# VectorE and ScalarE order at the norm boundaries of a two-layer trunk, and evictions of W_o moved ahead of weight splits

## The chip, the cores and the metric

One core of one Trainium2 chip. The metric is the device time of one execution in microseconds (us); a figure for a kernel is the median of several executions.

## The reference, cut to what matters

Two layers run over 272 tokens (16 learned ones and 256 given ones) with a model width of 1024, all in float32. Each layer has three sub-layers, each inside a pair of norms:

```
h = h + 0.5 * rmsnorm(swiglu(rmsnorm(h, g_pre), w1, w2), g_post)        # first half step
hn = rmsnorm(h, g_mix_pre)
u_pool, q, k, v, gate_pool, gate_attn = split(hn @ w_in)
merged = sigmoid(gate_pool) * y_pool + sigmoid(gate_attn) * y_attn
h = h + rmsnorm(merged @ w_o, g_mix_post)
h = h + 0.5 * rmsnorm(swiglu(rmsnorm(h, g_pre2), w3, w4), g_post2)      # second half step
```

The place where one sub-layer's result is normed and added to the trunk h, and the next sub-layer's operand is made from h, is called a boundary here.

## The kernel before, in words

The trunk `h` lies as 8 tiles (k = 0 to 7) of 128 features x 272 tokens. A float32 product is formed on TensorE from three products of rounded parts: each weight and each operand is split in a high part and a low part (`w_hi`, `w_lo`, `x_hi`, `x_lo`), and `products` (L437 to L439) issues high times high, high times low, and low times high. ScalarE makes the high parts (`split_hi` L833 for weights, `x_high` L857 for the operand), VectorE the low parts as source minus high part (`split_lo` L1076, `x_low` L1140).

Weights arrive in units of 1 MB or less, in a ring of four slots that SyncE fills. A slot's `raw` copy is free when VectorE has made its low part, its `w_hi` and `w_lo` when TensorE has used them. The order of the work on each engine is written out by hand, and semaphores tie the engines.

A boundary goes as follows. TensorE ends the last output tile; ScalarE squares it (`square`, L843); TensorE sums the squares over the features with one-column matmuls (`sum_part`, L513), with matmuls of no use around the waits (`keep_warm`, L523); ScalarE takes a root, VectorE refines it (`post_rms`, L1121 to L1129); TensorE spreads it over the partitions (`spread_rms`, L528). Then `boundary` runs on VectorE. For each tile it issues `normed` (L1149: `tmp` from `y` in SBUF and the spread root in PSUM), the update of `h` (L1158: `tmp` plus `h`, both in SBUF) and `x_low` (L1140: from `h` and `x_hi`, both in SBUF). ScalarE's `pre_norm` makes `x_hi` of each tile and the square of it, for the next norm. GpSimd adds up these squares (`add_squares`, L1536 for the first two, L1539 after that, SBUF to SBUF). `sq` has two buffers, and a square from the third on waits until an add has read its buffer. TensorE's `deep_pair` takes the 8 operand tiles in turn, twelve matmuls for each, and begins tile k when `x_lo` k is there; of tile 0 it takes the products with `x_hi` first (L457, L458).

In this program the boundary comes five times: after the first half step, after W_o and after the second half step of layer 0, and after the first half step and W_o of layer 1. What comes last is another path that the change does not touch. After a W_o boundary, and after the second half step, the next feed-forward stage begins: ScalarE loads an activation table, splits a unit of weights (`split_hi`), VectorE splits the first half of it and then computes the mean square (`split_lo_between` with `mean_square`, L1083, L1114), GpSimd takes the power -0.5 (`inverse_rms`, L1543), and TensorE spreads it (L528) between two output tiles. After the first half step, W_in follows, where VectorE computes the mean square before it splits weights.

W_o (units 62 to 65, output tiles 0 to 7) runs on TensorE as a `deep_pair` of units 62 and 63 and then units 64 and 65. VectorE evicts with `take_y` (L1444), two tiles of `y` each, and between them makes the low parts of units 66 to 68, the first weights of the next stage; ScalarE does their high parts and squares `y`. The last tile is squared straight from PSUM. The partial sum on TensorE ahead of the last three matmuls of tile 7 waits for GpSimd's fifth add, the one with the square of tile 5.

The core of `boundary` is:

```
for k in range(KD):
    dve.wait_ge(t_ready, ...)          # normed(k)
    h[:, k] = ...                      # L1158
    if k >= 2:
        x_low(at, columns, k - 1)
    if k + 1 < KD:
        normed(k + 1)
    if k == 0:
        x_low(at, columns, 0)
x_low(at, columns, KD - 1)
```

Of the kernel before, what the change touches and what calls it, by code (L numbers as in the profile page):

```python
# [48 lines left out]
KD = D // P  # L49
# [26 lines left out]
T_KV, T_Q, T_POOL, T_GATE, T_PP, T_AP, T_WO = 52, 56, 64, 68, 84, 92, 100  # L76
TILES = 160
# [6 lines left out]
TR0 = FFN_LAG - 4  # L84

NORMS = 6
# [7 lines left out]
def adds_to(n):  # L94

    return n // 2 * sum(ADDS) + n % 2 * ADDS[0]
# [38 lines left out]
def landed_at(u, layer, more=0):  # L135

    upto = sum(unit_dmas(v) for v in range(u % RING, u + 1, RING))
    return (layer * SLOT_DMAS[u % RING] + upto + more) * 16


def trunk(nc, x, meta_tokens, norm_g, ffn_w_in, ffn_w_out, w_in, pool_w_grp, pool_scale, w_pool_proj,
          sinks, w_attn_proj, w_o, geometry, out):
    with ExitStack() as ctx:
        def sb(name, shape, dt=F32):
            return ctx.enter_context(nc.sbuf_tensor(name, shape, dt))

        def sem(name):
            return ctx.enter_context(nc.semaphore(name))
# [8 lines left out]
        y = sb("y", [P, KD, T])  # L157
# [91 lines left out]
        tile_read = sem("tile_read")  # L249
# [575 lines left out]
        def _(act):  # L825
            act.sem_inc(silu_done, 2)

            def split_hi(u, l, more=0):
                act.wait_ge(raw_landed[u % RING], landed_at(u, l, more))

                act.wait_ge(unit_done, l * UNITS + u + 1 + (more * 4))
                for w, hi, _ in split_parts(u, l=l):
                    last = act.activation(hi, w, ACT.Copy)  # L833
                last.then_inc(hi_done, 1)

            def square(n, m, src, ready, at):

                act.wait_ge(ready, at)
                if m < 2:
                    act.wait_ge(ssq_done, n + 1)  # L840
                else:
                    act.wait_ge(acc_done, adds_to(n) + max(1, m - 2))
                act.activation(sq[:, m % 2, :], src, ACT.Square).then_inc(sq_done, 1)  # L843
# [11 lines left out]
            def x_high(columns, h_before, k):  # L855
                act.wait_ge(h_ready, h_before + k + 1)
                act.activation(x_hi[:, k, :], h[:, k, :], ACT.Copy, scale=columns[:, k:k + 1]).then_inc(xhi_ready, 1)  # L857

            def pre_norm(n, columns, h_before):

                for k in range(KD):
                    x_high(columns, h_before, k)
                    square(n, k, h[:, k, :], h_ready, h_before + k + 1)

            def silus(f, l, pair, more=0):
# [134 lines left out]
            for l in range(DEPTH):  # L1000
                ffn(0, l)
                act.wait_ge(layer_consts, l + 2)
                pre_norm(l * NORMS + 2, g_cur[:, 2 * KD:3 * KD], l * 3 * KD + KD)
                act.preload_act_table(ACT.Exp)
                for u in range(41, 46):
                    split_hi(u, l)
                act.wait_ge(v_turned, l + 1)
                act.activation(v_tok[:, :, :], pT_bank[:, :].rearrange("p (b c) -> p b c", b=2), ACT.Copy
                               ).then_inc(v_ready, 1)
                act.activation(v_pair[:, :, :], pTm_bank[0:4 * META, KV_DIM:2 * KV_DIM].rearrange("p (j c) -> p j c", j=2),  # L1010
                               ACT.Copy)
                act.activation(v_meta[:, :], pTm_bank[0:META, 0:KV_DIM], ACT.Copy).then_inc(v_ready, 1)
                for u in range(46, 49):
                    split_hi(u, l)
                if meta_queries(l):
                    act.wait_ge(s0_step, l * S0_STEPS + S0_SHIFTED)
                    act.activation(s0[0:META, :, 0:META], s0[0:META, :, 0:META], ACT.Exp)
                    act.activation(stats0[:, 2, :], stats0[:, 1, :], ACT.Exp).then_inc(s0_exp, 1)
                for c in range(KD):
                    split_hi(49 + c, l)  # L1020
                    if c >= 1:
                        tanh(2 * c - 2, l)
                        tanh(2 * c - 1, l)
                        take_pT(2 * c - 2, l)
                    exps(2 * c, l)
                    exps(2 * c + 1, l)
                    if c >= 1:
                        take_pT(2 * c - 1, l)
                split_hi(57, l)
                tanh(2 * KD - 2, l)  # L1030
                tanh(2 * KD - 1, l)
                take_pT(HEADS - 2, l)
                split_hi(58, l)
                take_pT(HEADS - 1, l)
                split_hi(59, l)
                split_hi(60, l)
                for n in range(4):
                    split_hi(61 + n, l)
                    if n >= 1:
                        merge_hi(2 * n - 2, l)  # L1040
                        merge_hi(2 * n - 1, l)
                merge_hi(6, l)
                merge_hi(7, l)
                act.preload_act_table(ACT.Sqrt)
                split_hi(65, l)
                split_hi(66, l)
                for m in range(4):
                    square(l * NORMS + 3, m, y[:, m, :], tile_read, l * TILES + T_WO + m + 1 + TR0)
                split_hi(67, l)
                for m in range(4, 6):  # L1050
                    square(l * NORMS + 3, m, y[:, m, :], tile_read, l * TILES + T_WO + m + 1 + TR0)
                split_hi(68, l)
                square(l * NORMS + 3, 6, y[:, 6, :], tile_read, l * TILES + T_WO + 6 + 1 + TR0)
                last_square(l * NORMS + 3, bank[3], l * UNITS + U_WO + 4 + RING)
                take_root(l * NORMS + 3)
                pre_norm(l * NORMS + 4, g_cur[:, 4 * KD:5 * KD], l * 3 * KD + 2 * KD)
                act.preload_act_table(ACT.Silu)
                ffn(1, l)
                if l < DEPTH - 1:

                    pre_norm(l * NORMS + NORMS, g_next, l * 3 * KD + 3 * KD)
                    act.preload_act_table(ACT.Silu)
# [6 lines left out]
        def _(dve):  # L1069
# [3 lines left out]
            def split_lo(u, l, more=0):  # L1073
                dve.wait_ge(hi_done, l * UNITS + u + 1 + more)
                for w, hi, lo in split_parts(u, l=l):
                    last = dve.tensor_tensor(lo, w, hi.bitcast(F32), ALU.subtract)  # L1076
                last.then_inc(lo_done, 1)
# [59 lines left out]
            def x_low(at, columns, k):  # L1137

                dve.wait_ge(xhi_ready, at + k + 1)
                dve.scalar_tensor_tensor(out=x_lo[:, k, :], in0=h[:, k, :], scalar=columns[:, k:k + 1],  # L1140
                                         in1=x_hi[:, k, :].bitcast(F32), op0=ALU.mult, op1=ALU.subtract
                                         ).then_inc(xlo_ready, 1)

            def boundary(n, l, at, columns):

                def normed(k):
                    dve.scalar_tensor_tensor(out=tmp[:, k % 2, 0:T], in0=y[:, k, :],  # L1149
                                             scalar=g_cur[:, (2 * n + 1) * KD + k:(2 * n + 1) * KD + k + 1],  # L1150
                                             in1=small[:, S_BC:S_BC + T], op0=ALU.mult, op1=ALU.mult
                                             ).then_inc(t_ready, 1)

                dve.wait_ge(bcast_done, l * NORMS + 2 * n + 2)
                normed(0)
                for k in range(KD):
                    dve.wait_ge(t_ready, l * 3 * KD + n * KD + k + 1)
                    dve.scalar_tensor_tensor(out=h[:, k, :], in0=tmp[:, k % 2, 0:T], scalar=1.0 if n == 1 else 0.5,  # L1158
                                             in1=h[:, k, :], op0=ALU.mult, op1=ALU.add).then_inc(h_ready, 1)
                    if k >= 2:  # L1160
                        x_low(at, columns, k - 1)
                    if k + 1 < KD:
                        normed(k + 1)
                    if k == 0:
                        x_low(at, columns, 0)
                x_low(at, columns, KD - 1)

            def take_gate(f, l, unit, mp=0):

# [213 lines left out]
            for l in range(DEPTH):  # L1383
# [55 lines left out]
                merge_lo(7, l)  # L1439
                split_lo(65, l)  # L1440

                def take_y(n):
                    b = 2 * (n % 2)
                    take(U_WO + n, F_WO + n, l, (b, b + 1), lambda j, ps: dve.tensor_copy(y[:, 2 * n + j, :], ps),  # L1444
                         (l * NORMS + 4) * KD if n == 3 else None, (lambda: split_lo(68, l)) if n == 3 else None)

                take_y(0)
                take_y(1)
                split_lo(66, l)
                split_lo(67, l)  # L1450
                take_y(2)
                take_y(3)
                post_rms(3, l)
# [210 lines left out]
```

## Time and profile before

| | us |
|---|---|
| median of 3 runs | 1229.23 |
| lowest and highest | 1226.35, 1229.56 |
| the profiled execution, its own time | 1229.71 |
| its span in the trace | 1227.6 |
| TensorE matmuls busy | 1200.9 (98%) |
| VectorE busy | 738.3 (60%) |
| ScalarE busy | 538.9 (44%) |
| GpSimd busy | 449.9 (37%) |

The time of the execution is the span and some 2 us around it. Busy times are sums over instructions, and TensorE's are modelled ends of pipelined matmuls. The boundaries' first `normed` starts at 224.74, 422.93, 630.78, 838.72 and 1028.57 us of the span.

### The profile page before, as it was taken

How to read it: one execution, taken by the hardware profiler on the slowest of the kernel's cores; microseconds unless marked ns; L12 is line 12 of the kernel's file. 1: busy time of each engine (PE TensorE's matmuls, PEld its weight loads, DVE VectorE, ACT ScalarE, POOL GpSimd, SP SyncE). 2: the span in 40 equal slices, each digit the busy share in tenths (PEclk: the TensorE clock that was granted, in tenths of full speed). 3: DMA queues.
4: the chain of work that ended last, by engine and by line, in shares of the span. 5: the costliest groups of instructions: out<-in, count | busy, mean ns of one | idle time of the engine just before them, and what ended most of it. 6: DMA issues, size and time to landing. Idle time of an engine off the chain costs nothing.

```text
span 1227.6 us, 23903 instructions
## 1 busy us (share of the span) xinstructions
PE 1200.9 (98%) x9364; PEld 1165.2 (95%) x9364; DVE 738.3 (60%) x1020; ACT 538.9 (44%) x747; POOL 449.9 (37%) x527
## 2 busy tenths in 40 slices
PE   6999999999999999999999999999999999999997
PEld 5999999999899999999999999999988998999986
DVE  4755444768866575553467554447678766755543
ACT  5433334535654453334344333345366645443441
POOL 2645411204512266452117454112054123755600
PEclk9999999999999899999999999999999999999999
DMA  9655356473256455534646553564733663664540
GB/s 286 207 171 162 119 171 205 116 231 104 70 138 206 137 165 179 171 120 152 206 139 207 171 162 117 171 205 117 232 104 83 167 198 104 212 199 155 169 173 35
DMA packets 197597, 197.58 MB, mean 161 GB/s; under 512 B 4120, under 2 KB 190720, under 8 KB 197520
## 3 DMA queue, kind: packets, MB, share of 16 engines
q1 hardware_dynamic: 197232, 196.22, 50.7%
q8 instruction: 56, 0.92, 0.3%
q10 hardware_dynamic: 288, 0.27, 0.1%
q14 instruction: 21, 0.17, 0.0%
HBM read 195.42 MB, written 1.05 MB: 160 GB/s over the span
## 4 chain that ended last, share of the span: by engine, by line
PE 86%; DVE 6%; ACT 4%; issue 2%; POOL 1%; DMA 0%; SPq 0%; DVEq 0%; ACTq 0%; POOLq 0%
PE bank L437 26%; PE bank L439 25%; PE bank L438 25%; ACT w_hi L833 2%; PE bank L619 2%; PE bank L620 2%; PE bank L618 2%; DVE w_lo L1076 2%; PE bank L513 1%; PE bank L523 1%; DVE s L1300 1%; DVE x_lo L1140 1%; DVE stats L1304 1%; DVE h L1158 1%; PE bank L707 1%
## 5 line engine op out<-in xcount | busy, mean ns | idle before, releaser
L1076 DVE TENSOR_TENSOR w_lo<-raw,w_hi 128x2048 fp32r<-128x2048 f32 (+3 forms) x208 | 439.0, 2116 | 285.3 <-ACT w_hi L833 285.3
L437 PE MATMUL bank<-x_hi,w_hi 128*128 128x272 f32 (+1 forms) x2028 | 589.2, 291 | 6.4 <-DVE w_lo L1076 4.4
L439 PE MATMUL bank<-x_hi,w_lo 128*128 128x272 f32 (+1 forms) x2028 | 582.6, 287 | 0.0
L438 PE MATMUL bank<-x_lo,w_hi 128*128 128x272 f32 (+1 forms) x2028 | 580.8, 286 | 0.0
L833 ACT ACTIVATE w_hi<-raw 128x2048 fp32r<-128x2048 f32 (+2 forms) x212 | 355.6, 1686 | 446.9 <-PE bank L439 435.1
L437 PEld LDWEIGHTS bank<-x_hi,w_hi 128*128 128x128 f32 x2028 | 383.2, 189 | 10.6 <-DVE w_lo L1076 4.8
L438 PEld LDWEIGHTS bank<-x_lo,w_hi 128*128 128x128 f32 x2028 | 383.2, 189 | 0.3
L439 PEld LDWEIGHTS bank<-x_hi,w_lo 128*128 128x128 f32 x2028 | 383.1, 189 | 0.0
L437 PE MATMUL bank<-hid_hi,w_hi 128*128 128x272 f32 x528 | 152.9, 290 | 0.0
L438 PE MATMUL bank<-hid_lo,w_hi 128*128 128x272 f32 x528 | 152.2, 288 | 0.0
L439 PE MATMUL bank<-hid_hi,w_lo 128*128 128x272 f32 x528 | 151.5, 287 | 0.0
L1554 POOL TENSOR_TENSOR hid_hi<-silu,up_r 128x272 f32 x88 | 76.3, 867 | 176.4 <-DVE up_r L1181 163.6
L1559 POOL TENSOR_TENSOR hid_lo<-hid_f,hid_hi 128x272 f32 x88 | 118.4, 1345 | 19.9 <-POOL hid_f L1556 19.9
L1556 POOL TENSOR_TENSOR hid_f<-silu,up_r 128x272 f32<-128x272 f32 x88 | 102.2, 1162 | 0.0
L438 PEld LDWEIGHTS bank<-hid_lo,w_hi 128*128 128x128 f32 x528 | 99.4, 188 | 0.0
L439 PEld LDWEIGHTS bank<-hid_hi,w_lo 128*128 128x128 f32 x528 | 99.3, 188 | 0.0
L437 PEld LDWEIGHTS bank<-hid_hi,w_hi 128*128 128x128 f32 x528 | 99.2, 188 | 0.0
L1539 POOL TENSOR_TENSOR acc<-acc,sq 128x272 f32<-128x272 f32 x56 | 44.3, 791 | 120.9 <-ACT sq L843 118.0
L1536 POOL TENSOR_TENSOR acc<-sq 128x272 f32<-128x272 f32 x11 | 14.6, 1328 | 169.6 <-ACT sq L843 169.6
L1181 DVE TENSOR_TENSOR up_r<-bank,r 128x272 f32<-128x272 f32 x88 | 37.7, 436 | 56.2 <-PE bank L439 56.2
L1174 DVE TENSOR_TENSOR gate_r<-bank,r 128x272 f32<-128x272 f32 x88 | 37.5, 434 | 38.3 <-PE bank L439 38.1
L1590 POOL TENSOR_TENSOR acc<-s,stats 128x16 f32<-128x16 f32 x64 | 18.9, 295 | 89.9 <-DVE stats L1317 89.9
(185 smaller groups left out, 1252.5 us busy)
## 6 DMA issues: line engine op xcount, KB each, us to landing
raw<-in_ffn_w_in SPq DMA_DIRECT2D x88, 1024.0 KB, 5.1
raw<-in_w_in SPq DMA_DIRECT2D x24, 1024.0 KB, 5.5
raw<-in_ffn_w_out SPq DMA_DIRECT2D x24, 768.0 KB, 4.4
raw<-in_ffn_w_out SPq DMA_DIRECT2D x24, 640.0 KB, 4.0
raw<-in_ffn_w_out SPq DMA_DIRECT2D x10, 1024.0 KB, 5.1
raw<-in_w_in SPq DMA_DIRECT2D x16, 512.0 KB, 4.8
raw<-in_w_attn_proj SPq DMA_DIRECT2D x32, 256.0 KB, 4.4
raw<-in_w_o SPq DMA_DIRECT2D x8, 1024.0 KB, 5.3
```

What stands on the lines that cost most here:

```text
L437: pe.matmul(ps[:, t0:T], w[0], a_hi[:, t0:T], start=start, stop=False)
L438: pe.matmul(ps[:, t0:T], w[0], a_lo[:, t0:T], start=False, stop=False)
L439: return pe.matmul(ps[:, t0:T], w[1], a_hi[:, t0:T], start=False, stop=stop)
L618: pe.matmul(ps[:, :], hid_hi[:, k, cols], w[0], start=k == 0, stop=False)
L833: last = act.activation(hi, w, ACT.Copy)
L1076: last = dve.tensor_tensor(lo, w, hi.bitcast(F32), ALU.subtract)
L1174: dve.tensor_tensor(gate_r[:, j, :], bank[4 * (unit // 2 % 2) + j][:, 0:T], r[:, :], ALU.mult).then_inc(tile_read, 1)
L1181: dve.tensor_tensor(up_r[:, j, :], bank[2 + j][:, 0:T], r[:, :], ALU.mult).then_inc(tile_read, 1)
L1539: pool.tensor_tensor(acc[:, :], acc[:, :], sq[:, m % 2, :], ALU.add).then_inc(acc_done, 1)
L1554: pool.tensor_tensor(hid_hi[:, ds(i * 2 + j, 1), :].rearrange("p o t -> p (o t)"), silu[:, j, :], up_r[:, j, :], ALU.mult).then_inc(hid_hi ...
L1556: pool.tensor_tensor(hid_f[:, j, :], silu[:, j, :], up_r[:, j, :], ALU.mult).then_inc(hf_ready, 1)
L1559: pool.tensor_tensor(hid_lo[:, ds(i * 2 + j, 1), :].rearrange("p o t -> p (o t)"), hid_f[:, j, :], hid_hi[:, ds(i * 2 + j, 1), :].rearrang ...
```

## The change: what it does, and the diff

Three things move; no instruction is added or taken away. In `pre_norm` ScalarE makes `x_hi` of tile k+1 before it squares tile k. In `boundary` VectorE updates `h` of tiles 0 and 1 before it makes `x_lo` 0, and from then on makes `x_lo` k in the same round as the update of `h` k, behind `normed` k+1. In W_o the low part of unit 67 goes from ahead of tile 4 to behind tile 6, and ScalarE's high part of unit 67 from ahead of the square of tile 4 to behind that of tile 5, and the square of tile 6 ahead of the high part of unit 68.

```diff
 def pre_norm(n, columns, h_before):
+    x_high(columns, h_before, 0)
     for k in range(KD):
-        x_high(columns, h_before, k)
+        if k + 1 < KD:
+            x_high(columns, h_before, k + 1)
         square(n, k, h[:, k, :], h_ready, h_before + k + 1)
...
 # ScalarE, W_o
-split_hi(67, l)
 for m in range(4, 6):
     square(l * NORMS + 3, m, ...)
+split_hi(67, l)
+square(l * NORMS + 3, 6, ...)
 split_hi(68, l)
-square(l * NORMS + 3, 6, ...)
...
 # VectorE, boundary
-    if k >= 2:
-        x_low(at, columns, k - 1)
+    if k == 1:
+        x_low(at, columns, 0)
     if k + 1 < KD:
         normed(k + 1)
-    if k == 0:
-        x_low(at, columns, 0)
-x_low(at, columns, KD - 1)
+    if k >= 1:
+        x_low(at, columns, k)
...
 # VectorE, W_o
+def split_two():
+    split_lo(67, l)
+    split_lo(68, l)
 def take_y(n):
-    take(..., (lambda: split_lo(68, l)) if n == 3 else None)
+    take(..., split_two if n == 3 else None)
 take_y(0)
 take_y(1)
 split_lo(66, l)
-split_lo(67, l)
 take_y(2)
 take_y(3)
```

On VectorE, the boundary before (`tmp` is `normed`, `h` the update, `x_lo` the low part):

```order
L1149 SCALAR_TENSOR_TENSOR tmp<-y,g_cur,bank 128x272
L1158 SCALAR_TENSOR_TENSOR h<-tmp,h 128x272
L1149 SCALAR_TENSOR_TENSOR tmp<-y,g_cur,bank 128x272
L1140 SCALAR_TENSOR_TENSOR x_lo<-h,g_cur,x_hi 128x272
L1158 SCALAR_TENSOR_TENSOR h<-tmp,h 128x272
L1149 SCALAR_TENSOR_TENSOR tmp<-y,g_cur,bank 128x272
L1158 SCALAR_TENSOR_TENSOR h<-tmp,h 128x272
L1140 SCALAR_TENSOR_TENSOR x_lo<-h,g_cur,x_hi 128x272
L1149 SCALAR_TENSOR_TENSOR tmp<-y,g_cur,bank 128x272
L1158 SCALAR_TENSOR_TENSOR h<-tmp,h 128x272
```

and the same place now (lines have moved by two):

```order
L1151 SCALAR_TENSOR_TENSOR tmp<-y,g_cur,bank 128x272
L1160 SCALAR_TENSOR_TENSOR h<-tmp,h 128x272
L1151 SCALAR_TENSOR_TENSOR tmp<-y,g_cur,bank 128x272
L1160 SCALAR_TENSOR_TENSOR h<-tmp,h 128x272
L1142 SCALAR_TENSOR_TENSOR x_lo<-h,g_cur,x_hi 128x272
L1151 SCALAR_TENSOR_TENSOR tmp<-y,g_cur,bank 128x272
L1142 SCALAR_TENSOR_TENSOR x_lo<-h,g_cur,x_hi 128x272
L1160 SCALAR_TENSOR_TENSOR h<-tmp,h 128x272
L1151 SCALAR_TENSOR_TENSOR tmp<-y,g_cur,bank 128x272
L1142 SCALAR_TENSOR_TENSOR x_lo<-h,g_cur,x_hi 128x272
```

Before, a round from tile 2 on is `h` k, `x_lo` k-1, `normed` k+1; now it is `h` k, `normed` k+1, `x_lo` k, so that `h` k+1 comes directly behind `x_lo` k.

On VectorE in W_o before (the first row is the low part of unit 65):

```order
L1076 TENSOR_TENSOR w_lo<-raw,w_hi 128x2048
L1444 COPY y<-bank 128x272 x4
L1076 TENSOR_TENSOR w_lo<-raw,w_hi 128x2048 x2
L1444 COPY y<-bank 128x272 x3
L1076 TENSOR_TENSOR w_lo<-raw,w_hi 128x2048
L1444 COPY y<-bank 128x272
```

and now:

```order
L1078 TENSOR_TENSOR w_lo<-raw,w_hi 128x2048
L1449 COPY y<-bank 128x272 x4
L1078 TENSOR_TENSOR w_lo<-raw,w_hi 128x2048
L1449 COPY y<-bank 128x272 x3
L1078 TENSOR_TENSOR w_lo<-raw,w_hi 128x2048 x2
L1449 COPY y<-bank 128x272
```

One weight split of 128x2048 has gone from ahead of the three evictions of tiles 4, 5 and 6 to behind them.

## Rows read from the trace of the kernel before

**Rows 1.** The page, part 4: share of the span by engine in the chain.
```profile
PE 86%; DVE 6%; ACT 4%; issue 2%; POOL 1%; DMA 0%; SPq 0%; DVEq 0%; ACTq 0%; POOLq 0%
```

**Rows 2.** Waits of PE: us in total, times, longest us.
```profile
PE bank L437 <- DVE x_lo L1140: 1.5, 4, 0.4
...
PE bank L513 <- POOL acc L1539: 1.1, 2, 0.9
```

**Rows 3.** Timeline, VectorE, first boundary: start, duration (us), instruction, idle before.
```profile
224.74 0.50 DVE L1149 SCALAR_TENSOR_TENSOR tmp<-y,g_cur,bank 128x272 f32<-128x272 f32 x1 [0.64 <-PE bank L528]
...
226.36 0.50 DVE L1140 SCALAR_TENSOR_TENSOR x_lo<-h,g_cur,x_hi 128x272 fp32r<-128x272 f32 x1 [0.24 <-ACT x_hi L857]
226.78 0.43 DVE L1158 SCALAR_TENSOR_TENSOR h<-tmp,h 128x272 f32<-128x272 f32 x1
...
228.02 0.49 DVE L1140 SCALAR_TENSOR_TENSOR x_lo<-h,g_cur,x_hi 128x272 fp32r<-128x272 f32 x1
...
230.29 0.52 DVE L1158 SCALAR_TENSOR_TENSOR h<-tmp,h 128x272 f32<-128x272 f32 x1
230.74 1.00 DVE L1140 SCALAR_TENSOR_TENSOR x_lo<-h,g_cur,x_hi 128x272 fp32r<-128x272 f32 x1
...
232.18 0.66 DVE L1158 SCALAR_TENSOR_TENSOR h<-tmp,h 128x272 f32<-128x272 f32 x1
...
236.75 0.50 DVE L1140 SCALAR_TENSOR_TENSOR x_lo<-h,g_cur,x_hi 128x272 fp32r<-128x272 f32 x1 [0.18 <-ACT x_hi L857]
```

**Rows 4.** Timeline, ScalarE, the same boundary.
```profile
225.81 0.52 ACT L857 ACTIVATE x_hi<-h,g_cur 128x272 fp32r<-128x272 f32 x1 [2.57 <-DVE h L1158]
...
227.25 0.52 ACT L857 ACTIVATE x_hi<-h,g_cur 128x272 fp32r<-128x272 f32 x1 [0.60 <-DVE h L1158]
```

**Rows 5.** Timeline, GpSimd, the same boundary.
```profile
228.17 0.97 POOL L1536 TENSOR_TENSOR acc<-sq 128x272 f32<-128x272 f32 x1 [22.22 <-ACT sq L843]
229.74 1.70 POOL L1539 TENSOR_TENSOR acc<-acc,sq 128x272 f32<-128x272 f32 x2 [0.60 <-ACT sq L843]
231.77 0.77 POOL L1539 TENSOR_TENSOR acc<-acc,sq 128x272 f32<-128x272 f32 x1 [0.33 <-ACT sq L843]
```

**Rows 6.** Timeline, TensorE, the same boundary: tile 5 begins; the sum behind tile 7.
```profile
235.11 0.39 PE L437 MATMUL bank<-x_hi,w_hi 128*128 128x272 f32 x1
...
239.73 0.72 PE L513 MATMUL bank<-ones,acc 128*128 128x1 f32 x6
```

**Rows 7.** Timeline, GpSimd and VectorE, a feed-forward stage of layer 0.
```profile
39.67 0.78 POOL L1559 TENSOR_TENSOR hid_lo<-hid_f,hid_hi 128x272 f32 x1 [0.23 <-POOL hid_f L1556]
...
39.72 2.87 DVE L1076 TENSOR_TENSOR w_lo<-raw,w_hi 128x2048 fp32r<-128x2048 f32 x1 [1.61 <-ACT w_hi L833]
```

**Rows 8.** Timeline, behind the W_o boundary of layer 0: ScalarE, GpSimd, TensorE.
```profile
435.17 1.28 ACT L1057 ACT_TABLE_LOAD   x1
...
439.79 1.77 POOL L1543 TENSOR_TENSOR rt<-var,half 128x3 f32<-128x3 f32 x1 [3.79 <-DVE var L1114]
...
441.62 0.54 PE L528 MATMUL bank<-ident,rt 128*128 128x128 f32 x3
```

**Rows 9.** Timeline, VectorE, W_o of layer 0: unit 67, ahead of tile 4.
```profile
411.14 2.29 DVE L1076 TENSOR_TENSOR w_lo<-raw,w_hi 128x2048 fp32r<-128x2048 f32 x1 [3.31 <-ACT w_hi L833]
```

**Rows 10.** Last sum and first `normed` of three boundaries; one stretch (third last column: PEclk).
```profile
222.11 0.83 PE L513 MATMUL bank<-ones,sq 128*128 128x1 f32 x6 [0.49 <-ACT sq L843]
...
418.59 1.31 PE L513 MATMUL bank<-ones,sq 128*128 128x1 f32 x6 [0.49 <-ACT sq L843]
...
422.93 0.50 DVE L1149 SCALAR_TENSOR_TENSOR tmp<-y,g_cur,bank 128x272 f32<-128x272 f32 x1 [1.85 <-PE bank L528]
...
1025.15 0.83 PE L513 MATMUL bank<-ones,sq 128*128 128x1 f32 x6 [0.49 <-ACT sq L843]
...
1028.57 0.50 DVE L1149 SCALAR_TENSOR_TENSOR tmp<-y,g_cur,bank 128x272 f32<-128x272 f32 x1 [1.42 <-PE bank L528]
...
420.00:422.00 2.00, 2.00 (x10) 2.00 (x11) 0.73 (x5) 0.20 (x1) 0.00 (x0) 0.50 0.88 293
```

More of the change, by code:

```diff
@@ L1048, in _ @@
                     square(l * NORMS + 3, m, y[:, m, :], tile_read, l * TILES + T_WO + m + 1 + TR0)
-                split_hi(67, l)
                 for m in range(4, 6):
                     square(l * NORMS + 3, m, y[:, m, :], tile_read, l * TILES + T_WO + m + 1 + TR0)
+                split_hi(67, l)
+                square(l * NORMS + 3, 6, y[:, 6, :], tile_read, l * TILES + T_WO + 6 + 1 + TR0)
                 split_hi(68, l)
-                square(l * NORMS + 3, 6, y[:, 6, :], tile_read, l * TILES + T_WO + 6 + 1 + TR0)
                 last_square(l * NORMS + 3, bank[3], l * UNITS + U_WO + 4 + RING)
@@ L1444, in take_y @@
                     take(U_WO + n, F_WO + n, l, (b, b + 1), lambda j, ps: dve.tensor_copy(y[:, 2 * n + j, :], ps),
-                         (l * NORMS + 4) * KD if n == 3 else None, (lambda: split_lo(68, l)) if n == 3 else None)
+                         (l * NORMS + 4) * KD if n == 3 else None, split_two if n == 3 else None)
                 take_y(0)
```

## The prediction

> **What bounds the kernel now.** I read the page first, then TensorE's waits, then the five boundaries on the timeline of each engine, and last W_o and the granted clock around it. In the chain that ended last TensorE has 86%, and VectorE and ScalarE together 10% [rows 1]: a change on those two is worth only what TensorE stops or starts to wait for. The list of waits shows how little that is. The waits for `x_lo` come to 1.5 us, and the waits of W_o's partial sum for GpSimd's adds to 1.1 us [rows 2]. So the gain is small whatever happens, and the question is what the new order does to engines that had a margin.
>
> At a boundary I take the first `normed` as time 0 (224.74 at the first [rows 3]). TensorE then needs an `x_lo` for each 12 matmuls, and three tiles and the slow first matmul take 239.73 - 235.11 = 4.62, or 1.54 a tile [rows 6]. Before, `x_lo` 1 ends at 3.77 and `x_lo` 7 at 12.51 [rows 3], TensorE's sum behind tile 7 comes at 14.99 [rows 6].
>
> **A lock between VectorE and GpSimd.** Three durations in the boundary are not those of their kind. An `x_lo` takes 0.49 and once 1.00, an update of `h` 0.43 and once 0.66 [rows 3]. GpSimd's add takes 0.77 and once 0.97 [rows 5]. The ends explain them. The add of 231.77 ends at 232.54 and the update of 232.18 at 232.84, 0.30 later. The pair of adds ends at 231.44 and the long `x_lo` at 231.74, again 0.30 later. The add of 0.97 ends at 229.14, which is 0.77 behind 228.37, and the `x_lo` beside it ends at 228.51, 0.14 later. So an update or an `x_lo` (two operands in SBUF) and an add run one after the other: VectorE lets go 0.14 before its recorded end, and an instruction of VectorE that had to wait ends 0.30 behind the add. `normed`, with one operand in PSUM, I take as free.
>
> **The new order, stepped through.** I count from the end of an update of `h` k. `x_hi` k starts 0.04 later (227.21 to 227.25 [rows 3, 4]), and `x_lo` k 0.55 behind that start (225.81 to 226.36), so at 0.59. The next update now stands directly behind `x_lo` and is issued 0.42 after it (226.36 to 226.78), at 1.01. On ScalarE the square of tile k-1 now follows `x_hi` k, and GpSimd's add for it starts 0.92 behind the start of `x_hi` (227.25 to 228.17 [rows 4, 5]), at 0.96. `x_lo` lets go at 0.59 + 0.49 - 0.14 = 0.94. So the add arrives when the lock is free, 0.05 ahead of the update, and holds it: the add ends at 1.73 and the update at 2.03. The next round repeats this. **A round takes 2.03 us, and TensorE needs one each 1.54 us.** Before, `x_lo` k-1 and `normed` stood between two updates, and the adds fell beside `normed` in most rounds.
>
> Does 0.05 decide? In the feed-forward stages GpSimd starts 0.02 to 0.05 ahead of a weight split 26 times. The first is the row of 39.67: the split, issued at 39.72, takes 2.87 [rows 7] where one alone takes 2.29 [rows 9], and the multiply keeps its 0.78. All 26, the last at 1059.18, go this way. And the second add of the pair began 0.77 before 231.44, at 230.67, 0.14 before the end of the update at 230.81 and ahead of the `x_lo` of 230.74 [rows 3, 5]: GpSimd does get in between two instructions of VectorE that follow each other.
>
> The opening of the new boundary is better than before: updates 0 and 1 end at 0.96 and 1.84, `x_lo` 1, behind `x_lo` 0 and `normed` 2, at 3.07 (0.70 sooner), `x_lo` 2 at 4.51. The first add, at 4.39, then meets update 3, due at 4.43: the add ends at 5.16, the update at 5.46, `x_lo` 3 at 5.46 + 0.59 + 0.49 = 6.54. From there `x_lo` 4 to 7 end 2.03 apart, at 8.57, 10.60, 12.63 and 14.66. TensorE ends one tile behind the last: 14.66 + 0.06 + 1.6 = 16.3, or **1.4 us later** than 14.99.
>
> **What follows a boundary.** Update 7 ends at 13.58, `x_hi` 7 starts at 13.62, and two squares follow it, 0.4 each: ScalarE is done at about 14.80, where before the table load began at 435.17 - 422.93 = 12.24 [rows 8, 10]. Behind it hang the table load, the high part, half a low part, the mean square and GpSimd's power, which ended at 441.56, and TensorE spread it at 441.62 [rows 8]. This path had no margin, and now it is 14.8 - 12.2 = 2.6 later. So at the three boundaries into a feed-forward stage (two W_o, one second half step) TensorE is **2.5 us** later and not 1.4. At the two into W_in the mean square waits for TensorE's sum alone, and 1.4 stands. Sum: 2 x 1.4 + 3 x 2.5 = **+10.3 us**.
>
> **W_o.** Unit 67's low part (2.29 [rows 9]) leaves the place ahead of tile 4. Tiles 4 and 5 are evicted when TensorE has them, their squares and adds come some 3 us sooner, and the partial sum waits for no add: **-1.1 us** [rows 2]. The square of tile 6 comes some 2 us sooner too. The moved splits end near 418.4 in layer 0, and the eviction of tile 7 follows the last square as before. Units 67 and 68 are first used after the boundary. SyncE loads the unit that follows 67 some 2.6 us later, into a slot that is not used for over 20 us. I cost these at nothing, with that time as cover.
>
> **The clock.** From 420.00 to 422.00 the granted clock is 0.50, so 1.2 GHz in place of 2.4 [rows 10], after TensorE had only one-column matmuls and short waits for most of 416 to 419. From the last sum to the first `normed` the first boundary takes 224.74 - 222.11 = 2.63, the W_o boundaries 4.34 and 3.42 [rows 10]. The surplus of 1.7 and 0.8 is the clock's. The change shortens the sparse stretch by 0.2 and 0.9 and shifts it in time. Between 0 and -2.5 I take half, **-1.2 us**. The Trainium skill ("TensorE: Matmul & The Clock Gate", What's actually happening) has the clock fall back only after an idle window; by that no wait here, of 0.9 at most [rows 2], would lower it, nothing could be won, and the sum would be 1238.9. The trace disagrees with it, since the clock did fall.
>
> **Sum.** The profiled execution took 1229.7, half a microsecond above the median of 1229.23. 1229.7 + 10.3 - 1.1 - 1.2 = 1237.7; against the median I say **1237.5 us**. A measurement of this kernel can tell about 0.3%, or 3.7 us, from no change.
>
> **The rivals.** *VectorE first.* If the update wins against the add, a round takes 0.59 + 0.42 + 0.44 = 1.45, less than TensorE's 1.54, and the add has room beside `normed`. `x_lo` 7 would end at 11.7 in place of 12.5, for some -0.8 at each boundary into W_in, and ScalarE's last square at 11.85 in place of 12.24, for -0.4 at the three others. With W_o and the clock: 1229.7 - 1.6 - 1.2 - 1.1 - 1.2 = 1224.6, faster. It decides once the add arrives over 0.05 later against the update than the rows say. For it speaks how narrow that is; against it the 26 cases. The Trainium skill's page "SBUF — State Buffer", Who interferes with whom, has the first to issue hold the pair of ports for the whole instruction. By that `x_lo` would hold it until 1.08, the update be in the queue by then, and 1224.6 could result. The trace disagrees as to the last 0.14 of an instruction (the add at 230.67). *Mixed.* The race goes either way from tile to tile. Each lost one costs 0.6, five are run at each boundary, and at half of them lost the time is near 1231. *W_o gives nothing.* Were the sum's wait replaced by one for the square of tile 6, +1.1 and 1238.8; it lies inside the forecast.
>
> **Chances.** GpSimd first everywhere 0.72 (of which 0.25 for a clock that gives nothing, at 1238.9); VectorE first 0.18; mixed 0.10. The forecast's own range is 1234 to 1241: the clock's ends give +1.2 and -1.3; a boundary whose clock falls because TensorE now idles there would add 0.8 each, so some +2 more at the top; less delay behind the boundary than 2.5 takes 2 off. The range of 8 in 10 goes on down over the mixed case to 1225. Faster by over 0.3%: 0.19. Within: 0.06. Slower: 0.75.
>
> **What would show it.** In the new trace updates of `h` 3 to 7 last about 1.03 us in place of 0.44, `x_lo` ends come 2.03 apart, adds keep 0.77, TensorE waits for `x_lo` some 25 times (9 us or so in all), and for GpSimd's power by about 1 us three times; the wait for an add in W_o is gone. Updates of 0.44, 1.45 us apart, with adds stretched to about 1.0, would show the first rival. A forecast of slower is wrong if the last `x_lo` ends before 12.5 us after the first `normed`.

## The result, and the profile after

The changed kernel takes 1238.12 us (median of 4 runs, 1237.48 to 1238.68), where the kernel before took 1228.47 (median of 4, 1226.35 to 1229.56) beside it. The ratio is 1.0078, with a 95% interval from 1.0062 to 1.0094: slower by 0.8%. The profiled execution took 1237.94, with a span of 1235.8. The forecast was 1237.5.

TensorE's waits in the changed kernel (line, what it waited for: us in total, times, longest us):

```profile
PE bank L437 <- DVE x_lo L1142: 6.0, 23, 0.4
...
PE bank L528 <- POOL rt L1547: 3.2, 3, 1.2
PE bank L513 <- ACT sq L843: 2.4, 5, 0.5
...
PE bank L457 <- ACT x_hi L857: 1.5, 3, 0.6
PE bank L437 <- DVE kT L1391: 0.5, 1, 0.5
```

The waits for `x_lo` were 1.5 us and the waits for the adds in W_o 1.1 [rows 2]. The first are now 6.0 and the second are gone. Two others cost time now: the waits for GpSimd's power (`rt`), 3.2 us at three places where there were 0.3 at one, and one for the eviction of K (`kT`).

The timeline of VectorE at the first boundary (start, duration in us, instruction, idle before), where the first `normed` starts at 224.67:

```profile
227.68 0.43 DVE L1160 SCALAR_TENSOR_TENSOR h<-tmp,h 128x272 f32<-128x272 f32 x1
228.03 0.49 DVE L1151 SCALAR_TENSOR_TENSOR tmp<-y,g_cur,bank 128x272 f32<-128x272 f32 x1
228.70 0.50 DVE L1142 SCALAR_TENSOR_TENSOR x_lo<-h,g_cur,x_hi 128x272 fp32r<-128x272 f32 x1 [0.18 <-ACT x_hi L857]
229.12 1.02 DVE L1160 SCALAR_TENSOR_TENSOR h<-tmp,h 128x272 f32<-128x272 f32 x1
230.06 0.48 DVE L1151 SCALAR_TENSOR_TENSOR tmp<-y,g_cur,bank 128x272 f32<-128x272 f32 x1
230.73 0.50 DVE L1142 SCALAR_TENSOR_TENSOR x_lo<-h,g_cur,x_hi 128x272 fp32r<-128x272 f32 x1 [0.18 <-ACT x_hi L857]
231.15 1.01 DVE L1160 SCALAR_TENSOR_TENSOR h<-tmp,h 128x272 f32<-128x272 f32 x1
...
238.80 0.50 DVE L1142 SCALAR_TENSOR_TENSOR x_lo<-h,g_cur,x_hi 128x272 fp32r<-128x272 f32 x1 [0.59 <-ACT x_hi L857]
```

GpSimd beside it:

```profile
229.07 0.77 POOL L1540 TENSOR_TENSOR acc<-sq 128x272 f32<-128x272 f32 x1 [24.30 <-ACT sq L843]
231.09 0.76 POOL L1543 TENSOR_TENSOR acc<-acc,sq 128x272 f32<-128x272 f32 x1 [1.25 <-ACT sq L843]
```

Updates are counted from 0 by their tile, so the row of 227.68 is update 2. It takes 0.43. Update 3 is issued at 229.12, and the first add has started at 229.07, 0.05 earlier. The add takes its usual 0.77 and ends at 229.84. The update ends at 230.14, 0.30 later, so that it takes 1.02. From then on each update from tile 3 to tile 7 has its add about 0.05 ahead of it: the updates start 2.01 to 2.03 us apart and take 1.0. It is so at all five boundaries, for 25 of the 40 updates, and in none of these rounds do the two engines fall out of step. The median duration of all 40 updates is 1.00, where before it was 0.46.

TensorE at the end of that boundary, and the path of the power behind the W_o boundary of layer 0 (TensorE, ScalarE, GpSimd):

```profile
240.95 0.77 PE L513 MATMUL bank<-ones,acc 128*128 128x1 f32 x6
...
437.17 1.28 ACT L1059 ACT_TABLE_LOAD   x1
...
441.79 1.77 POOL L1547 TENSOR_TENSOR rt<-var,half 128x3 f32<-128x3 f32 x1 [3.21 <-DVE var L1116]
...
443.61 0.54 PE L528 MATMUL bank<-ident,rt 128*128 128x128 f32 x3 [1.02 <-POOL rt L1547]
```

The sum comes 240.95 - 224.67 = 16.28 us behind the first `normed`, not 14.99 [rows 3, 6]. At the second boundary the first `normed` is at 422.41, so the table load starts at 14.76, where it was 12.24 [rows 8, 10], and TensorE waits 1.02 for the power, where it did not wait at 441.62 [rows 8].

All five boundaries, measured in us from start to start on the timelines: A from TensorE's last sum to the first `normed` (2.63 where the clock holds), B from there to the sum behind tile 7, C from that sum to the spread of the next norm.

```
            boundary 1          2                   3                   4                   5
            A     B     C       A     B     C       A     B     C       A     B     C       A     B     C
before      2.63 14.99  3.69    4.34 14.93  3.76    2.63 14.94  3.83    2.63 15.01  3.50    3.42 14.79  3.92
changed     3.74 16.28  3.74    2.63 16.29  4.91    3.39 16.29  4.98    3.00 16.28  3.56    2.63 16.22  4.98
```

The difference of the spans, 8.2 us, comes apart so: B gives +6.7 and C +3.5, together **+10.2**. A, the clock's share, gives -0.3. From the spread of the next norm behind boundaries 1 and 4, with which C ends, to the first partial sum of W_o it is 0.0 and -0.35, and within W_o's sums -0.15. The first stage, ahead of everything that was changed, was 1.2 shorter in this execution.

### The profile page after: what moved, and what is told of

The parts are those of the page before. It is cut to its first block, busy times and chain, and to the rows that moved or that the text cites. A ratio compares the mean times of both kernels' runs of the same rounds, so it can differ in the third digit from the quotient of the medians.

```text
span 1235.8 us, 23903 instructions
## 1 busy us (share of the span) xinstructions
PE 1203.0 (97%) x9364; PEld 1164.8 (94%) x9364; DVE 744.6 (60%) x1020; ACT 539.2 (44%) x747; POOL 445.1 (36%) x527
## 4 chain that ended last, share of the span: by engine, by line
PE 82%; DVE 9%; ACT 5%; issue 3%; POOL 1%; DMA 0%; SPq 0%; DVEq 0%; ACTq 0%; POOLq 0%
PE bank L437 24%; PE bank L439 24%; PE bank L438 24%; DVE h L1160 2%; ACT w_hi L833 2%; DVE w_lo L1078 2%; PE bank L620 2%; PE bank L619 2%; PE bank L618 2%; DVE x_lo L1142 1%; ACT x_hi L857 1%; PE bank L513 1%; DVE s L1301 1%; PE bank L523 1%; DVE stats L1305 1%
```

## The experiments

Medians in us, each beside runs of the kernel before on the same chip. The changed kernel was not run again beside them, so a difference from its 1238.12 is one between sessions; the medians of the kernel before were 1228.47 beside the changed kernel, and 1229.35 to 1229.67 in the others. The diffs are cut short. "Stepped" in the expectations means the same walk through the order, with the same lock, as in the prediction.

**The boundary part alone.** W_o's evictions, splits and squares as before.

```diff
 # VectorE and ScalarE, W_o: the changed kernel's edit undone
-square 4, 5; split_hi(67); square 6; split_hi(68)
+split_hi(67); square 4, 5; split_hi(68); square 6
-take_y(0); take_y(1); split_lo(66); take_y(2); y 6; split_lo(67); split_lo(68); y 7
+take_y(0); take_y(1); split_lo(66); split_lo(67); take_y(2); y 6; split_lo(68); y 7
```

> The boundary part of the change alone (both engines' new order), W_o as before. Theory (GpSimd's add gets the lock 0.05 us ahead of the update of h): updates 3 to 7 of each boundary take 1.00 us, the sum behind tile 7 comes 16.3 us after the first normed instead of 14.9, TensorE waits about 1.2 us for GpSimd's power three times, and the time is 10 us above before, about 1238.5 us, since the W_o part gave back at most 1. Rival (most of the loss comes from W_o or from a clock that falls elsewhere): within 4 us of before.

Measured: 1241.23 against 1229.35, ratio 1.0097 (1.0078 to 1.0117). B is 16.2 to 16.3 at all five boundaries, and the waits for the power come to 3.2. The loss lies in the boundary. It is more than forecast, 11.9 and not 10. W_o, which is as before here, has no part in that. The traces show two things that I had not counted: between boundaries 1 and 4 and W_o 0.4 and 0.8 are lost, and the parts A are 3.0 longer in all than before. This kernel is 3.1 above the changed one; in the traces 1.7 of the difference is W_o's and 3.2 the parts A's, in an execution of 1243.15, 1.9 above its median.

**The W_o part alone.** The boundaries as before.

> The W_o part alone. Theory: the waits of the partial sum for the adds (0.20 and 0.94 us) go, -1.1 us, and the clock changes where it falls, -2 to +1: 1226.5 to 1229.5 us. Rival (the evictions moved ahead cost the next stage, so that the part loses): over 1230 us, with a new wait of TensorE for w_lo of unit 67 or 68.

Measured: 1226.83 against 1229.35, ratio 0.998 (0.9969 to 0.999), so some 2.5 us faster: within the range, and no wait for `w_lo` of a later unit appears. From the spread behind boundary 1 to the first partial sum of W_o it takes 172.34 in place of 172.74, and in layer 1 164.41 in place of 165.51: -1.5, with another -0.15 within the sums. The other 0.9 of the 2.5 lies in no path that I read; the interval reaches from -3.8 to -1.2.

**ScalarE as before, VectorE new.**

```diff
-x_high(columns, h_before, 0)
 for k in range(KD):
-    if k + 1 < KD:
-        x_high(columns, h_before, k + 1)
+    x_high(columns, h_before, k)
     square(n, k, ...)
```

> The change with ScalarE's order of before (x_hi k, then the square of k), VectorE's order new. Stepped through with the same lock rule: the add of tile k then arrives with x_lo k or just ahead of the next update, the rounds of 2.03 us begin one tile earlier (update 2 already takes about 1.0), the sum comes 16.9 us after the first normed, and the last square ends at 15.0: about 2 x 0.6 + 3 x 0.2 = 1.8 us above the changed kernel, near 1240 us. Rival (the new order of ScalarE, which puts the squares late, is what brings the add against the update): with the old order the updates take 0.44, and the time is near or below before.

Measured: 1238.97 against 1229.35, ratio 1.008 (1.006 to 1.01). B is 16.87, 16.85, 16.84, 16.85 and, at the last boundary, 15.66; the stepped figure was 16.9. The time is near that of the changed kernel (1238.12 in another session) and 1 below the expected one. The timelines of VectorE and GpSimd at the first boundary:

```profile
227.72 1.01 DVE L1158 SCALAR_TENSOR_TENSOR h<-tmp,h 128x272 f32<-128x272 f32 x1
...
229.74 1.01 DVE L1158 SCALAR_TENSOR_TENSOR h<-tmp,h 128x272 f32<-128x272 f32 x1
```

```profile
227.52 0.91 POOL L1538 TENSOR_TENSOR acc<-sq 128x272 f32<-128x272 f32 x1 [22.01 <-ACT sq L843]
229.69 0.77 POOL L1541 TENSOR_TENSOR acc<-acc,sq 128x272 f32<-128x272 f32 x1 [1.26 <-ACT sq L843]
```

Here update 2 already waits, and from update 3 on the add is again 0.05 ahead. The place of the squares is thus not what brings the adds against the updates. It is VectorE's order, in which an update follows `x_lo` directly.

The last boundary shows how narrow it is. The first add, GpSimd's first row above, starts beside an `x_lo`, 2.81 behind the first `normed`, at all five boundaries. At four of them it takes 0.91 and update 2 waits. At the last one update 2 gets in first:

```profile
1039.18 0.44 DVE L1158 SCALAR_TENSOR_TENSOR h<-tmp,h 128x272 f32<-128x272 f32 x1
1038.99 1.26 POOL L1538 TENSOR_TENSOR acc<-sq 128x272 f32<-128x272 f32 x1 [10.27 <-ACT sq L843]
```

The rounds of 2 us begin only at update 4 there. So in one kernel the same tie went both ways.

**The adds a little later.** Two memsets of 48 columns on GpSimd, of no use, ahead of each add of a pre-norm (not of the post-norm sums); all else as in the changed kernel.

```diff
+def linger(q):
+    if q % 2 == 0:
+        pool.memset(spare[:, 0:48], 0.0)
+        pool.memset(spare[:, 48:96], 0.0)
 ...
+linger(q)
 pool.tensor_tensor(acc[:, :], ..., ALU.add)
```

> The changed kernel with two small memsets on GpSimd ahead of each add of a boundary's pre-norm squares, so that the add comes 0.1 us or more later against the update of h. If the race for the lock is what costs the time, VectorE now comes first: updates take 0.44 and follow each other by 1.45 us, adds stretch to about 1.0 us, the sum comes about 13.9 us after the first normed, the last square ends at 11.85, and the time falls by some 13 us below the changed kernel, to 1224.5 (1222.5 to 1226.5), below before too. Rival (the loss comes from the waits of x_lo for x_hi in the new order, not from the lock): the memsets change nothing or cost 1 to 3 us more, 1238 to 1241 us.

Measured: 1223.68 (1223.23 to 1225.92) against 1229.35, ratio 0.9958 (0.9943 to 0.9972). **Work added to GpSimd takes 14.4 us off the changed kernel (15.3 if each is taken against the kernel before beside it), and the result is 5.7 below the kernel before.** Its timeline, VectorE and then GpSimd:

```profile
230.44 0.44 DVE L1161 SCALAR_TENSOR_TENSOR h<-tmp,h 128x272 f32<-128x272 f32 x1
230.79 0.49 DVE L1152 SCALAR_TENSOR_TENSOR tmp<-y,g_cur,bank 128x272 f32<-128x272 f32 x1
231.47 0.50 DVE L1143 SCALAR_TENSOR_TENSOR x_lo<-h,g_cur,x_hi 128x272 fp32r<-128x272 f32 x1 [0.18 <-ACT x_hi L858]
231.89 0.43 DVE L1161 SCALAR_TENSOR_TENSOR h<-tmp,h 128x272 f32<-128x272 f32 x1
```

```profile
231.81 0.14 POOL L1538 MEMSET spare<- 128x48 f32 x1 [0.22 <-ACT sq L844]
231.88 0.14 POOL L1539 MEMSET spare<- 128x48 f32 x1
231.98 0.98 POOL L1551 TENSOR_TENSOR acc<-acc,sq 128x272 f32<-128x272 f32 x1
```

The round is 231.89 - 230.44 = 1.45, the update takes 0.43, and now the add waits: it ends at 232.96, which is 0.77 behind 232.19, and the update ends at 232.32, 0.13 later. B is 13.7 to 13.9. The rival, by which the waits of `x_lo` for `x_hi` (0.18 a round, still there) cost the time, has fallen.

**How little later.** One memset of one column.

```diff
-        pool.memset(spare[:, 0:48], 0.0)
-        pool.memset(spare[:, 48:96], 0.0)
+        pool.memset(spare[:, 0:1], 0.0)
```

> The changed kernel with one memset of a single column ahead of each add, to see how narrow the race is. The add came 0.05 us ahead of the update. If the memset shifts it by more than that (a guess: 0.07), VectorE comes first in every round and the time is that of the longer delay, near 1224 us. If by less, nothing changes: 1238 us. A race that goes either way from round to round would give a time between, near 1231 us, with updates of both lengths.

Measured: 1223.67 (1223.3 to 1223.99) against 1229.58, ratio 0.9951 (0.9937 to 0.9966): level with the two longer memsets, and with them the fastest of the study. VectorE and GpSimd:

```profile
228.69 0.44 DVE L1161 SCALAR_TENSOR_TENSOR h<-tmp,h 128x272 f32<-128x272 f32 x1
```

```profile
228.61 0.10 POOL L1538 MEMSET spare<- 128x1 f32 x1 [23.14 <-ACT sq L844]
228.67 1.09 POOL L1546 TENSOR_TENSOR acc<-sq 128x272 f32<-128x272 f32 x1
```

The first `normed` is at 224.23 here, so the add starts 4.44 behind it, where it was 4.40 (229.07 - 224.67) in the changed kernel: a shift of 0.04 us in the record is enough, and at all five boundaries. The add's record even begins 0.02 ahead of the update's, and the update wins. In the same trace a multiply of GpSimd that starts at 143.01, 0.02 ahead of a weight split of 128x1280, is not held up (0.78), and the split takes 2.11 where the one of 549.48 in the kernel before takes 1.49. A start in the record tells who comes first only to some hundredths of a microsecond.

**The boundary part with the adds later.** W_o as before, one memset of one column.

> The boundary part alone, with the single-column memset ahead of each add, so that VectorE wins the race; W_o as before. It parts the gain of the new boundary from that of W_o. Theory: W_o is worth 2.5 us (the W_o part alone: 1226.8 against 1229.4), so about 1226.2 us, between 1225 and 1227.5, still some 3 us below before. Rival (the gain of the late adds depends on W_o's order too): outside that.

Measured: 1226.78 against 1229.67, ratio 0.9976 (0.9967 to 0.9986). The new boundary, with the race won by VectorE, gives 2.9 us of its own. With W_o's 2.5 that is 5.4, near the 5.9 of the kernel above. The memset ahead of the adds with the boundary's old order was not run, so how much of the 2.9 is the new order's is open: before, too, some instructions waited (`x_lo` of 1.00, updates of 0.66 [rows 3]).

**The mean square first.** The changed kernel, with the path behind the boundary shortened.

```diff
-split_lo_between(u0 + 3, l, lambda: mean_square(4 * f, l))
+mean_square(4 * f, l)
+split_lo(u0 + 3, l)
```

> The changed kernel, but at a feed-forward stage VectorE computes the mean square ahead of the first weight split and not between its halves. Theory (three boundaries lose 1.1 us each beyond the rounds, because the path over ScalarE's table load and weight split to GpSimd's power ends 2.6 us later): with the mean square off that path TensorE waits no more for the power, the 3.2 us of those waits go, and the time is near 1235 us. Rival (that time is lost anyway, since the weight splits are late too and TensorE then waits for w_lo or a bank): 1237 us or more, with new waits in place of the old.

Measured: 1238.55 against 1229.58, ratio 1.0069 (1.0054 to 1.0085): no gain. TensorE's waits:

```profile
PE bank L437 <- DVE x_lo L1142: 6.0, 23, 0.3
...
PE bank L437 <- DVE up_r L1182: 2.2, 3, 1.0
```

The waits for the power are gone, C is 3.6 to 3.8, and a wait for the eviction of the second unit (`up_r`) has come in their place: it stands behind two weight splits, which come from ScalarE as late as before. So my expectation failed and its rival held. The lateness of ScalarE's splits reaches TensorE by two paths, and to remove one uncovers the other. On the timelines the three boundaries with what follows them are 1.0 shorter in all; the median does not show it.

**Both.** The adds late (two memsets) and the mean square first.

> The adds late and the mean square first. If both effects are what they seem, they add: 1223.7 less the 2.3 us that TensorE waited for the power there, 1221.4 us (1220 to 1223), some 8 us below before. Rival (what follows is bound by the weight splits): 1223 to 1225 us.

Measured: 1224.1 against 1229.58, ratio 0.9955 (0.9944 to 0.9967). It does not add up to 1221.4, and the rival's range (1223 to 1225) holds: the waits for the power (2.3) are gone and 1.3 for `up_r` have come. The clock fell at boundaries 4 and 5, which is no more than in the kernels with the late adds alone.

**W_o's partial sums apart.** One memset, and the first partial sum ahead of tile 7.

```diff
+sum_part(3, l, 0)                  # now ahead of tile 7
 def sums_so_far():                 # ahead of its last three matmuls
-    sum_part(3, l, 0)
     sum_part(3, l, 1)
```

> The changed kernel with the single-column memset, and W_o's first partial sum (of GpSimd's adds) moved from ahead of the last three matmuls of tile 7 to ahead of tile 7, as the feed-forward output has it, so that the one-column matmuls do not stand in one stretch. Theory (the clock falls at W_o because of that sparse stretch): from the last sum to the first normed both W_o boundaries take 2.6 us in place of 3.1 to 4.3, and the time falls by up to 1.5 us, to 1222.2. Rival (when the clock falls is a matter of when the program comes to a boundary, and of little else): 1223 to 1224.5 us, with the fall at other boundaries.

Measured: 1224.14 against 1229.67, ratio 0.9959 (0.9945 to 0.9973), no gain. A is 2.64 and 2.62 at the two W_o boundaries, as expected, but 3.31, 3.48 and 3.61 at the three others, where the code is the same as in kernels that had 2.63 there. Both statements come true in part, and the time is that of the rival. It is one trace.

## Why the prediction was right

**The lock.** This step carried the forecast, and it held to a few hundredths: updates of 1.00 to 1.02 for a stepped 1.03, rounds of 2.01 to 2.03 for 2.03, adds of 0.76 to 0.77, the last `x_lo` at 14.63 (238.80 + 0.50 - 224.67) for 14.66, TensorE's sum at 16.28 for 16.3. That the lock, and who comes first to it, is the cause and not a companion is shown by the two kernels with memsets. They leave every instruction of VectorE and ScalarE as it was, change who comes first, and take 14.4 us off. The rival of VectorE first, at 1224.6, is what those kernels measure, at 1223.7.

The odds rested on less than the text says. The 26 cases with a lead of 0.02 to 0.05 are there and all go to GpSimd. But seven weight splits of the kernel before start within 0.01 of a multiply of GpSimd, and these go either way: four (549.48, 561.59, 757.42, 769.53) come first and take 1.49, and the multiply takes 2.12. The memset shows how near the change lay to that: 0.04 in the record. That GpSimd would win was forecast from rows; that it did so in all 25 rounds is partly luck. A smaller slip: each of the "once" in the prediction (1.00, 0.66, 0.97) stands twice at the first boundary.

The waits for `x_lo` came 23 times for 25, but the list gives 6.0 and not "9 us or so". It counts from the modelled end of the matmul before. From start to start, less the 0.13 at which these matmuls otherwise follow each other, the same 23 come to 9.6.

As to the Trainium skill's page "SBUF — State Buffer" (Who interferes with whom), the exclusive hold is as it says in the rows shown here, but for the last 0.14 of an instruction, as the prediction had it: at the first boundary `x_lo` runs from 228.70 to 229.20, and the add begins at 229.07 and takes no longer than 0.77.

**What follows a boundary.** 2.5 at the three boundaries into a feed-forward stage was B and C together: measured 1.36 + 1.15, 1.35 + 1.15 and 1.43 + 1.06. Right, and in all +10.2 for +10.3. The path I named (the power) is the one that the profile shows. The experiment with the mean square adds that a second path, the splits and the eviction behind them, lies only 0.2 to 0.4 us a boundary behind it.

**The two boundaries into W_in.** "1.4 stands" was too good. The mean square did follow TensorE's sum, but the weight splits behind it did not:

```profile
241.75 0.16 DVE L1116 TENSOR_SCALAR var<-bank 128x3 f32<-128x3 f32 x1 [2.46 <-PE bank L513]
242.75 4.63 DVE L1078 TENSOR_TENSOR w_lo<-raw,w_hi 128x1024 fp32r<-128x1024 f32 x4 [0.84 <-ACT w_hi L833]
...
247.77 0.79 DVE L1391 TENSOR_TENSOR kT<-bank,r 128x272 f32<-128x272 f32 x2
```

(VectorE behind the first boundary.) They wait 0.84 for ScalarE, which came with the lateness of its last square, and the eviction of K follows them. In layer 1 TensorE's next matmul into a bank that it frees waits 0.53 for it; in layer 0 the same matmul starts 0.37 later than before, and the other 0.07 is lost at the one behind it. The boundary part costs 0.4 and 0.8 between those boundaries and W_o (173.12 against 172.74, and 166.28 against 165.51, in the kernel with the boundary part alone). I had costed this at nothing.

**W_o.** -1.1 was too small: the part alone gives -1.65 on the paths, as above. The removed waits of 0.20 and 0.94 are in it, and the other 0.5 lies at the same place. In layer 0 before, and then in the kernel with the W_o part alone:

```profile
415.67 0.29 PE L439 MATMUL bank<-x_hi,w_lo 128*128 128x272 f32 x1
416.16 0.80 PE L513 MATMUL bank<-ones,acc 128*128 128x1 f32 x6 [0.20 <-POOL acc L1539]
```

```profile
415.92 0.29 PE L439 MATMUL bank<-x_hi,w_lo 128*128 128x272 f32 x1
416.04 0.72 PE L513 MATMUL bank<-ones,acc 128*128 128x1 f32 x6
```

The sum started 0.49 behind the last matmul and now starts 0.12 behind it, so the wait cost 0.37. The idle time of 0.20 is counted from the modelled end of the matmul, and is 0.16 short. In layer 1 it is 1.22 and 0.12, so 1.10 for a recorded 0.94. The rest is 0.08 less in the group of sums itself in each layer (0.80 and 0.72). Taking the listed idle for the cost was the error, and it cancels a part of the one on W_in.

**The clock.** Here the size was off. I took half of the surplus of 2.5, -1.2; it is -0.3. At W_o the fall is gone in this trace, as a granted clock of 1.00 in the stretch of rows 10 shows, but it has come to the boundaries behind the feed-forward output:

```profile
222.00:224.00 2.00, 2.00 (x12) 2.00 (x11) 0.73 (x5) 0.06 (x1) 0.00 (x0) 0.50 0.95 282
420.00:422.00 2.00, 2.00 (x18) 1.81 (x18) 1.09 (x7) 0.27 (x1) 0.00 (x0) 1.00 1.08 375
```

(Busy time by engine in two stretches of the changed kernel, granted clock in the last column but two.) Ahead of the first boundary no instruction was moved. Over the eleven traces of this study A exceeds 2.63 by 0.4 to 1.8 us somewhere in each, at W_o boundaries more often and by more than at the others, and the total lies between 2.1 and 5.5; so a single trace does not price it. Five of the traces have the same instructions up to the first boundary. The clock fell there in the three that came to the last sum at 220.93, 221.25 and 221.68, and held in the two that came at 222.11 and 222.38. That looks like a matter of when the program comes by. But with the mean square first it came at 222.41 and the clock fell (A 3.19), and in the kernel with both it came at 222.41 as well and the clock held (2.63). What sets the moment is open. As to the Trainium skill's page "TensorE: Matmul & The Clock Gate" (What's actually happening), its idle window, taken as the prediction takes it, is against these rows too: the clock fell where TensorE had waits of 0.2 to 0.9 and one-column matmuls. The same section also has the clock follow how busy the engine has been, and that the rows do not contradict.

The sum thus came out within 0.6 us of the measured median, with its largest term right and three small ones wrong, by +1.2, -0.5 and +0.9. These make +1.6, and a first stage that happened to be 1.2 shorter hid most of it: the mechanism was right, and that it was right to 0.6 us is luck.

## What to carry to other kernels

Where VectorE and GpSimd run a chain in step, look in the trace for two instructions with two operands in SBUF that start within a tenth of a microsecond, and work out who gets in first: here such a tie repeated in every round and cost some 0.6 us each time. An order that looks better by dependences can lose such a race, and a useless short instruction on the engine off the path won it back here. And an operand that comes later at a boundary also delays what ScalarE does next, so follow that engine's next weight split to TensorE before pricing the boundary. And price a wait of TensorE from start to start: the listed idle time was 0.16 us short of the cost of each.

## What the runs showed that I had not expected

One memset of a single column, which moved the add by 0.04 us, turned 1238.1 into 1223.7 us: 1.2% of the time from a race at 25 places. The recorded starts do not decide it alone, since the add's record began 0.02 ahead and it lost, while beside weight splits in the same trace GpSimd won with the same lead. The clock fell at other boundaries from kernel to kernel, at the first one too, ahead of which nothing had been moved.
